# Two transformer blocks on one core: layers written out in one program, an eight-slot weight ring, biases as two rounded parts

## The reference

```python
for l in range(2):                                   # block 1
    h = rms_norm(x, mix_norm_g[l]); proj = h @ w_in[l]          # 1024 -> 4352
    y_sb  = stick_breaking_attention(sb_q, sb_k, sb_v) @ w_branch_sb[l]      # 8 heads of 64
    y_swa = sliding_window_sink_attention(rope(norm(q)), rope(norm(k)), v, sinks[l]) @ w_branch_swa[l]
    x = x + (sigmoid(gate0) * y_sb + sigmoid(gate1) * y_swa) @ w_out[l]
    x = x + square(relu(rms_norm(x, mlp_norm_g[l]) @ w_up[l])) @ w_down[l]   # 4096 wide
for l in range(2):                                   # block 2, a = sqrt(2)
    x = layer_norm(a*x + 0.5 * swiglu(x, ffn1...[l]), ln1[l])                # 2816 wide
    z = x @ w_in[l] + b_in[l]
    x = layer_norm(a*x + (gmlp, short convolution, latent attention, sparse attention,
                          each gated and projected, summed) @ w_o[l], ln2[l])
    x = layer_norm(a*x + cross_attention(x, mem, ...), ln3[l])
    x = layer_norm(a*x + 0.5 * swiglu(x, ffn2...[l]), ln4[l])
```

## Time and profile before

| | |
|---|---|
| runs, us | 2544.78, 2547.96, 2545.2 (median 2545.2) |
| profiled execution | 2547.4 us, of which 2545.8 us span |
| TensorE busy | 2383.2 us, 94% |
| TensorE weight loads | 86% |
| VectorE busy | 1436.7 us, 56% |
| ScalarE busy | 1146.0 us, 45% |
| GpSimd busy | 280.7 us, 11% |
| granted TensorE clock, mean | 0.968 of full |
| read from DRAM | 391 MB, 154 GB/s over the span |

### The profile page before, as it was taken

How to read it: one execution, slowest core, us unless ns; L and a number is a source line. 1 busy time by engine, 2 the same in 40 slices (tenths; PEclk the granted TensorE clock), 3 DMA queues, 4 the chain that set the end, 5 groups by cost and what they waited for, 6 DMA issues and landing times.

```text
span 2545.8 us, 42947 instructions
## 1 busy us (share of the span) xinstructions
PE 2383.2 (94%) x16386; PEld 2185.5 (86%) x16386; DVE 1436.7 (56%) x1842; ACT 1146.0 (45%) x1792; POOL 280.7 (11%) x228
## 2 busy tenths in 40 slices
PE   6988998998999899999998989979999999998997
PEld 6978986887998898799997889879978999887996
DVE  4556555545654444655466764454464555677445
ACT  4744543573553444445343444434444534354443
POOL 0001210000120110100002221121110000132111
PEclk9998998999999999899998999989999999999998
DMA  6423554432454555344433435645644434143552
GB/s 202 139 94 116 182 190 144 166 117 100 149 190 141 216 183 198 145 154 166 150 117 107 175 116 183 206 152 185 205 138 181 161 117 166 67 166 119 197 201 97
DMA packets 56851, 394.47 MB, mean 155 GB/s; under 512 B 6678, under 2 KB 7040, under 8 KB 10944
## 3 DMA queue, kind: packets, MB, share of 16 engines
q1 hardware_dynamic: 52864, 377.98, 42.7%
q0 software_dynamic: 3776, 13.64, 1.7%
HBM read 391.24 MB, written 1.05 MB: 154 GB/s over the span
## 4 chain that ended last, share of the span: by engine, by line
PE 57%; DVE 4%; issue 4%; ACT 2%; DMA 1%; POOL 0%; DVEq 0%; SPq 0%; ACTq 0%; POOLq 0%
PE psum L372 50%; PE psum L721 2%; PE psum L691 2%; DVE w_low L330 1%; PE psum L1565 1%; PE psum L705 1%; ACT w_high L327 1%; PE psum L398 1%; PE psum L576 1%; DMA ring<-in_weights 1%; DVE xs L1852 0%; DVE mx L747 0%; ACT attn_p L803 0%; PE psum L683 0%; DVE gates L610 0%
## 5 line engine op out<-in xcount | busy, mean ns | idle before, releaser
L330 DVE TENSOR_TENSOR w_low<-ring,w_high 128x1024 fp32r<-128x1024 f32 x704 | 923.8, 1340 | 613.7 <-ACT w_high L327 613.0
L372 PE MATMUL psum<-xT_high,w_high 128*128 128x256 f32 x3168 | 908.0, 287 | 22.0 <-DVE w_low L330 14.9
L327 ACT ACTIVATE w_high<-ring 128x1024 fp32r<-128x1024 f32 x704 | 718.2, 1052 | 428.9 <-PE psum L372 388.2
L372 PE MATMUL psum<-xT_low,w_high 128*128 128x256 f32 x3168 | 902.2, 285 | 0.0
L372 PE MATMUL psum<-xT_high,w_low 128*128 128x256 f32 x3168 | 901.9, 285 | 0.0
L372 PEld LDWEIGHTS psum<-xT_high,w_high 128*128 128x128 f32 x3168 | 614.5, 194 | 24.6 <-issue 18.9
L372 PEld LDWEIGHTS psum<-xT_low,w_high 128*128 128x128 f32 x3168 | 614.5, 194 | 0.2
L372 PEld LDWEIGHTS psum<-xT_high,w_low 128*128 128x128 f32 x3168 | 613.9, 194 | 0.0
L372 PE MATMUL psum<-w_high,hidden 128*128 128x512 f32 x1216 | 378.0, 390 | 9.7 <-DVE attn_pT L1841 5.2
L372 PEld LDWEIGHTS psum<-w_high,hidden 128*128 128x128 f32 x1216 | 228.2, 188 | 60.7 <-issue 11.8
L372 PE MATMUL psum<-w_low,hidden 128*128 128x512 f32 x608 | 236.6, 389 | 0.0
(11 more groups left out here) (212 smaller groups left out, 2279.9 us busy)
## 6 DMA issues: line engine op xcount, KB each, us to landing
ring<-in_weights SPq DMA_DIRECT2D x354, 1024.0 KB, 4.9
pages<-in_affine POOLq DMA_DIRECT2D x16, 512.0 KB, 6.5
ring<-in_weights SPq DMA_DIRECT2D x4, 880.0 KB, 4.4
pages<-in_mem POOLq DMA_DIRECT2D x2, 1024.0 KB, 5.2
x<-in_x_in SPq DMA_DIRECT2D x1, 1024.0 KB, 4.8
pages<-in_rows POOLq DMA_DIRECT2D x2, 512.0 KB, 7.3
y<-x SPq DMA_DIRECT2D x1, 1024.0 KB, 4.1
masks<-in_masks POOLq DMA_DIRECT2D x1, 640.0 KB, 8.2
```

What stands on the lines that cost most here:

```text
L327: eng.activation(high, raw, ACT.Copy).then_inc(*self.flag("w_rounded").one())
L330: eng.tensor_tensor(self.w_low[:, q % SPLITS, 0:w], raw, high.bitcast(F32), ALU.subtract).then_inc(*self.flag("w_split").one())
L372: m = pe.matmul(out, a, b, start=(first and i == 0), stop=(last and i == len(pairs) - 1))
```

## The change

**Program.** There is one part instead of four, without the barriers between them. The two layers are written out one behind the other, so that every wait is on a constant. x is loaded in two transfers, one for each half of the tokens, and the norm of a half waits for its transfer alone. The parameters of block 1 (`cols_1`, `rows_1`) are loaded once for both layers, at the start. The four adds of "down" move into the statistics of the next layer's norm; behind the second layer of block 1 they stay by themselves. Block 2 waits for these four adds. Two small tables of block 2 go through GpSimd's queue instead of SyncE's.

**Weights.** All four layers are one sequence of pieces of 1024 columns (512 KB a transfer), in eight slots. `w_low` is written over the raw piece in its slot, so a slot is free when TensorE has read the piece. `w_high` has six places. At the end of a layer, and before each norm, the splits go two pieces further than before, inside a norm three.

**Last norm.** In the last layer VectorE alone computes y from statistics, gain and bias (`last_norm`), and y is stored in four transfers of 128x512.

**Biases.** The bias row is rounded by ScalarE into row 0 of a 33-row operand and its rest written by VectorE into row 32, in the first feed-forward part of each layer (at groups 4 and 6); the other rows are zeroed by GpSimd. One fp32r matmul by a constant with ones in rows 0 and 32 (`pick`) adds both for one half of the tokens.

**Masks and compressors.** For the second half of the tokens the causal mask is added behind the scores, on the diagonal half of the columns alone (24 matmuls of 512 columns become 256). In the compressors i is now the outer loop and g the inner one.

```diff
-CHUNK = 2048
-SLOTS = 3
-SPLITS = 4
+SLOTS = 8
+SPLITS = 6
+TAIL = 4
...
+    def load_weights(self, sp, flat):
+        for piece in range(w.first[self.section], w.first[self.section] + len(stream.widths)):
+            width = w.pieces[piece][0]
+            if piece >= SLOTS:
+                sp.wait_ge(*w.released[piece - SLOTS])
...
+                eng.tensor_tensor(self.w_low[:, piece % SLOTS, 0:width], raw, high.bitcast(F32), ALU.subtract
+                                  ).then_inc(self.flag("w_split").sem, 1)
...
+        late = mask is not None and w == 2 * P and a["mask_late"]
...
+        if late:
+            m = pe.matmul(region.rearrange("p (h w) -> p h w", w=w)[:, :, P:w], self.identb[:, :],
+                          self.masks[:, 0, 0:len(heads) * P], start=False, stop=True, skip_group_check=True)
...
-        with dve.Fori(0, DEPTH) as l:
+        for l in c.layers(1):
...
-            c.norm_vector(dve, l, c.x, False, RMS_EPS)
+            c.norm_vector(dve, l, c.x, False, RMS_EPS, first_rows if l == 0 else lambda t, n: add("down", l - 1, t, n))
...
-            split(c.piece_after["down"])
+            split(c.piece_after["down"] + 2)
...
+            def bias_high():
+                act.activation(bias_parts[0:1, :], bias_row, ACT.Copy).then_inc(*c.flag("bias_rounded").one())
...
+            def bias_low():
+                dve.tensor_tensor(bias_parts[32:33, :], bias_row, bias_parts[0:1, :].bitcast(F32), ALU.subtract
+                                  ).then_inc(*c.flag("bias_parted").one())
...
-                for g in range(2):
-                    for i in range(32):
+                for i in range(32):
+                    for g in range(2):
...
+            def last_norm(l):
+                    for cut in halves:
+                        dve.scalar_tensor_tensor(c.xs[:, t, cut], c.xs[:, t, cut], mean, gain[:, cut],
+                                                 ALU.subtract, ALU.mult).then_inc(*step.one())
+                    dve.wait_ge(*c.flag("std_ready").at(l, c.flag("var_ready").made))
+                    dve.reciprocal(inverse, std).then_inc(*step.one())
+                    for cut in halves:
+                        dve.scalar_tensor_tensor(c.x[:, t, cut], c.xs[:, t, cut], inverse, bias[:, cut],
+                                                 ALU.mult, ALU.add).then_inc(c.flag("y_ready").sem, 1)
...
-                sp.dma_start(io["y"].rearrange("t p d -> p t d"), c.x[:, :, :]).then_inc(c.flag("stored").sem, 16)
+                for i in range(2 * NT):
+                    sp.dma_start(io["y"][t, :, cut], c.x[:, t, cut]).then_inc(c.flag("stored").sem, 16)
```

More of the change, by code:

```diff
@@ L307, in open_weights, with layers @@
[L307 to L322, removed]
+    def layers(self, block):
+        start = {name: flag.made for name, flag in self.flags.items()}
+        for l in range(DEPTH):
+            for name, flag in self.flags.items():
+                flag.made = start.get(name, 0)
+            self.section = (block - 1) * DEPTH + l
+            self.rotated = None
+            yield l
@@ new lines, in _ @@
+            split(c.piece_after["out"] + 2)
+            c.norm_vector(dve, l, c.x, False, RMS_EPS, lambda t, n: add("out", l, t, n))
+            split(c.piece_after["out"] + 3)
+            c.norm_evacuate(dve, l, 1, "dve", c.cols_1[:, l, KD:2 * KD])
+            split(c.piece_after["out"] + SPLITS)
+            for n in range(16):
+                c.wait_drained(dve, l, banks, ("up", n))
+                if n >= 2:
+                    dve.wait_ge(*c.flag("hidden").at(l, n - 1))
+                dve.tensor_tensor(c.attn_pT[:, n % 2, :], c.attn_p[:, n % 2, :], c.attn_p[:, n % 2, :],
+                                  ALU.mult).then_inc(*c.flag("hidden_whole").one())
+                after(("up", n))
@@ L1296, in _ @@
+            split(c.piece_after["down"] + 2)
+        for t in range(NT):
+            for n in range(2):
+                add("down", DEPTH - 1, t, n)
     @block.gpsimd
     def _(pool):
-        pool.wait_ge(c.flag("loaded").sem, c.loads * 16)
-        with pool.Fori(0, DEPTH) as l:
-            pool.wait_ge(*c.flag(f"drained{banks.groups['down', 1, 1][1]}").at(l, 0))
-            pool.dma_start(cols[:, :], io["cols_1"][bass.ds(l, 1), :, :].rearrange("o p w -> (o p) w")
-                           ).then_inc(c.flag("params").sem, 16)
-            pool.dma_start(rows[:, :], io["rows_1"][bass.ds(l, 1), :].to_broadcast([P, 2 * HD + 8])
-                           ).then_inc(c.flag("params").sem, 16)
+        for l in c.layers(1):
@@ L1311, in _ @@
             c.low_hidden(pool, l, KF1, 2, 0)
+    c.x_added = {}
+    for t in range(NT):
+        for n in range(2):
+            _, b, use = banks.groups["down", t, n]
+            c.x_added[t, n] = c.flag(f"drained{b}").at(DEPTH - 1, use + 1)
     @block.sync
     def _(sp):
-        with sp.Fori(0, DEPTH) as l:
-            c.load_weights(sp, l, stream, io["weights_1"])
+        for l in c.layers(1):
+            c.load_weights(sp, io["weights_1"])
 C_LN = 0
@@ L1480, in _ @@
             m.then_inc(input_turned.sem, 1)
[L1481 removed]
+        for l in c.layers(2):
             def pairs(key, act, kn, n_groups):
@@ L1555, in _ @@
             pe.wait_ge(*c.flag("blocks_ready").at(l, 4))
-            compressors = [c.weight(pe, l, stream, key) for key in ("cmpk", "cmpv")]
+            compressors = [[c.weight(pe, l, stream, (key, half)) for half in range(2)] for key in ("cmpk", "cmpv")]
             pe.wait_ge(*c.flag("n_roped").at(l, 2))
```

528 lines of the change are left out of this document (271 added, 257 removed).

## The result

The changed kernel takes 2472.6 us (median of four runs, 2468.8 to 2474.9), the one before 2546.6 (2544.8 to 2550.5). The ratio is 0.971, 95% interval 0.969 to 0.972: 71 to 79 us less. I had predicted 62 less. The direction and most terms were about right, but the gain is some 12 us larger than forecast: at the ratio of 0.9706, the 2545.2 us on which I based the forecast become 2470, just under the range of 2472 to 2502.

The account below looks back on a forecast made before the run. TensorE, busy 94% of the span, was taken as the bound. Ten terms summed to 62.0 us off the profiled 2547.4, giving 2485.4, and 2.2 less for the median: 2483 us, range 2472 to 2502.

Parts of the forecast that it names:

- Biases: Bias matmul pairs in two layers: fp32r saves 1.45 us on each of seven pairs, 10.2 us.
- 1.6 by the clock: Slow matmul groups behind layer 0's bias pairs: half of 3.3 us counted as gained, since the evidence was divided.
- Start: Kernel start: x in halves and gain columns asked for first bring the first product to 14.4, 9.3 us less.
- the first weights come late: Kernel start: late parameters, identity or first weights would shrink the 9.3 us gain, bounded by 5 and 11.
- The other gaps: Between layers of block 1, between blocks, between layers of block 2, at the end: 7.7, 4.2, 2.7 and 9.5 us less.
- gaps that don't close: Rival, chance 0.13: another wait stands behind each barrier or late weight; half of the five gaps' 33.4 us lost, 2500.
- Masks: 24 of the 48 masks with 512 columns halve: 2.6 us less, bounds 0 and 3.
- ten small waits: TensorE's waits for `w_low` inside the layers: 3.7 us in all gained, bounds 0 and 3.7.
- Compressors: Alternating partition halves and PSUM banks overlap, four records taking 140 ns for 222: 10.5 us less, ends 0 and 14.2.
- no overlap: Rival, chance 0.24: the partition halves don't overlap, the compressors gain nothing, and the kernel takes 2494 us.
- Starvation: Rival, chance 0.04: the weight ring starves TensorE, 2571 us at a landing of 16.8; 11 us of slack spoke against.

Follow-up runs that it names:

- the repeated pair: The changed kernel and the kernel before, each executed once more with nothing changed: spans 2470.8 and 2543.6 us.
- run 7: Changed kernel with group outside in compressors, one-row float32 biases, no splits beyond a layer's end and adds of down apart: span 2510.9 us, 39.7 more.
- run 10: Changed kernel with later first weight split, block 2's layers starting on input quarters, GpSimd's x work delayed: 2464.3 us, ratio 0.967 to the kernel before.

## Why the prediction was right and wrong

The step that failed is the last half sentence under "Biases": "and 1.6 by the clock". I looked for the clock only behind the bias pairs, because the earlier trace rows showed two slow groups there, and gave every other term its duration at a fixed clock. The trace of before had 65.6 us of half-speed cost in some thirty stretches, most of them behind a stall of TensorE. The change removed or shortened stalls at five places and the one-row matmuls, and 12.5 us of half-speed cost went (10.0 in the repeated pair; 13.6 and 13.9 by the second count); undoing four edits brought 11.2 back (run 7). Without this term the sum of the others was right to 0.2 us. That is luck: it holds errors of both signs, up to 3.6 us.

- **Start, 9.3 for 5.7.** Statistics at 4.72 for 4.4 were right. The bound named in the text, "the first weights come late", is what happened, by 3.6, and moving the split behind the copy won 1.9 to 3.2 of it back, by the execution that it is compared with (run 10).
- **The other gaps.** 7.7, 4.2, 2.7 and 9.5 came out as 7.4, 5.0, 2.8 and 10.6. The rival of gaps that don't close falls. Reading a gap's new length from the same chain elsewhere worked.
- **Biases.** 1.25 a pair for 1.45. The first pair of layer 0 saved nothing, as said; the same holds for the first of layer 1 but for 1.6 us that it had lost to the lower clock. So six pairs and not seven, 7.5 + 1.6 − 0.2 = 8.9.
- **Masks, waits.** 2.5 for 2.6. The ten small waits are gone, and gave 5.3 for 3.7, over the upper bound: I had counted the idle time alone.
- **Compressors, 10.5 for 12.4.** Overlap is full; the 28 ns I added to each change of half aren't there. The argument that spoke against it was misread: heads that share a bank in one unit are every second one, so all use the same partition half. Those 282 ns of the earlier trace rows never showed alternating halves, and the chance of 0.24 for no overlap rested on nothing. The trace of before did hold the answer: in the middle of each block of 128, where group 0 ends and group 1 begins, the records are 6, 50, 15 and 40 ns apart instead of 56.
- **Starvation.** It did not happen, but the bound was wrong. With seven slots 13 us are lost and with six 139, so the kernel stood one slot from a loss and not 11 us away. The error lies in the slack's arithmetic: seven pieces' time was taken for the lead, where a transfer has only the slots that the split lead leaves.

## What to carry to other kernels

Before summing gains on a matrix-engine-bound kernel, add up what the lower clock costs over the whole trace and ask of every removed stall which slow stretch stands behind it; here that was a sixth of the gain. For a ring of buffers the margin is the number of slots less the lead at which the next engine's program asks for them, and what a late slot costs depends on what stands behind the wait in that engine's program. Small matmuls like these, on half of the rows, took twice the time when neighbours didn't alternate between halves and banks.

## What the runs showed of the hardware

- Two float32 matmuls with 64x15 weights in different partition halves and PSUM banks start 7 ns apart and run together: 56 ns for two records of 64 columns instead of 112.
- A float32 matmul pair with one active row takes 1.91 us like one with 33, but only behind one-row pairs, two of four in each layer, did the granted clock fall to 0.51 for 3 us.
- VectorE's subtraction of two 128x512 tiles took 3.48 us beside GpSimd's adds on x, 1.29 without them.
- 512 KB land in 3.4 us and 1024 KB in 4.9. The Trainium skill ("DMA: Bandwidth & Descriptors", Bandwidth) advises 1 MiB or more. In the changed kernel's trace TensorE never waits for a weight transfer, and ScalarE does for 27.3 us in all; no run tried 1024 KB in it.
